# A hybrid decoder layer on one core: the up product by seven products in place of eight over half of its inner dimension

## What is computed

```python
def hybrid_layer(x, ...):
    ...                                        # projections, short convolution, attention, merge
    x = x + merged @ w_out
    f = rmsnorm(x, norm2_w) @ w_up             # the up product, 1024 -> 4096
    x = x + jnp.square(jax.nn.relu(f)) @ w_down   # the down product, 4096 -> 1024
    return x, new_conv, k, v
```

## Time and profile before

| | |
|---|---|
| median of 3 runs | 1617.1 us (1617.06 to 1617.59) |
| the profiled execution's own time | 1616.8 us |
| its span, first to last instruction | 1615.1 us |
| mean granted TensorE clock | 0.998 of 2.4 GHz |
| matmuls | 9776 |
| up product of a cycle | 23.72 us |
| down product of a cycle | 20.90 us |

### The profile page before, as it was taken

How to read it: one execution, slowest core, us unless ns; L and a number is a source line. 1 busy time by engine, 2 the same in 40 slices (tenths; PEclk the granted TensorE clock), 3 DMA queues, 4 the chain that set the end, 5 groups by cost and what they waited for, 6 DMA issues and landing times.

```text
span 1615.1 us, 25413 instructions
## 1 busy us (share of the span) xinstructions
PE 1600.1 (99%) x9776; PEld 1483.0 (92%) x9776; DVE 1059.5 (66%) x1411; ACT 530.9 (33%) x1044; POOL 720.7 (45%) x594
## 2 busy tenths in 40 slices
PE   9999999999999999999999999999999999999997
PEld 8999999999998888999988989999999999999996
DVE  7685977859612221356433587877777887787777
ACT  6655665555522221332134411111111111111123
POOL 5212121121222111223687486666666776666661
PEclk9999999999999999999999999999999999999999
DMA  4201112011184767363354111110011111111012
GB/s 165 68 27 55 54 40 68 27 41 54 41 283 149 233 221 238 118 232 104 122 189 144 53 53 52 53 53 26 27 53 53 52 53 53 53 53 53 27 40 111
DMA packets 133491, 144.99 MB, mean 90 GB/s; under 512 B 7839, under 2 KB 98619, under 8 KB 133372
## 3 DMA queue, kind: packets, MB, share of 16 engines
q1 hardware_dynamic: 133226, 143.34, 27.5%
q10 hardware_dynamic: 146, 0.04, 0.0%
HBM read 124.37 MB, written 18.98 MB: 89 GB/s over the span
## 4 chain that ended last, share of the span: by engine, by line
PE 85%; DVE 9%; ACT 3%; issue 1%; DMA 0%; DVEq 0%; ACTq 0%
PE ps L1289 51%; PE ps L1623 6%; PE ps L1625 6%; PE ps L1624 6%; DVE sp L2114 2%; PE ps L1580 2%; PE ps L1585 2%; PE ps L1583 2%; PE ps L1483 2%; DVE zc L2106 1%; PE ps L1439 1%; PE ps L1449 1%; PE ps L1527 1%; PE ps L1495 1%; ACT sp L1797 1%
## 5 line engine op out<-in xcount | busy, mean ns | idle before, releaser
L1289 PE MATMUL ps<-xh,wh 128*128 128x352 f32 (+1 forms) x956 | 322.6, 337 | 0.9 <-DVE xl L2087 0.7
L1289 PE MATMUL ps<-xh,wl 128*128 128x352 f32 (+1 forms) x956 | 312.7, 327 | 0.0
L1289 PE MATMUL ps<-xl,wh 128*128 128x352 f32 (+1 forms) x956 | 312.4, 327 | 0.0
L2243 DVE TENSOR_TENSOR x<-ps,x 128x1024 f32<-128x1024 f32 x210 | 257.1, 1224 | 42.8 <-PE ps L1625 23.9
L1140 POOL CAST wh<-raw 128x1024 fp32r<-128x1024 f32 x48 | 50.3, 1047 | 478.3 <-issue 205.4
L1289 PE MATMUL ps<-yh,wl 128*128 128x384 f32 (+1 forms) x768 | 250.6, 326 | 0.0
L1289 PE MATMUL ps<-yh,wh 128*128 128x384 f32 (+1 forms) x768 | 250.6, 326 | 0.0
L1289 PE MATMUL ps<-yl,wh 128*128 128x384 f32 (+1 forms) x768 | 250.3, 326 | 0.0
L1921 ACT ACTIVATE hf<-hf 128x384 f32<-128x384 f32 (+1 forms) x96 | 48.6, 508 | 554.7 <-DVE hf L2296 554.7
L1289 PEld LDWEIGHTS ps<-xh,wh 128*128 128x128 f32 x956 | 179.8, 188 | 17.2 <-issue 15.5
L1289 PEld LDWEIGHTS ps<-xl,wh 128*128 128x128 f32 x956 | 180.0, 188 | 0.7
(11 more groups left out here) (213 smaller groups left out, 3141.8 us busy)
## 6 DMA issues: line engine op xcount, KB each, us to landing
raw<-in_w_in SPq DMA_DIRECT2D x80, 256.0 KB, 3.3
...
```

The source lines that it names most:

```text
L1289: ins = mm(out, lhs[:, k * P:(k + 1) * P], rhs[:, x], start=(first and a == 0 and m == 0), stop=(last and a == n - 1 and m == 2))
L2243: V_.tensor_tensor(x, src, x, ALU.add).then_inc(step_free, 1)
```

## The change

Pairs 1 to 15 of the up product get a new form. Of the 8 K tiles, tiles 0 to 3 go by seven products in place of eight: the 2 x 2 of y is (K tiles 0-1, K tiles 2-3) x (first, second half of the prompt tokens), that of w_up is (tile of hidden channels) x (K tiles 0-1, 2-3). Tiles 4 to 7 stay plain, in chunks of 512 tokens, and the 64 sample tokens get matmuls of their own for all 8 tiles. Entries `("mix", n, m)`, m = 0 to 8, take the place of the six `("up", ...)`. A partial sum that several results need stays in its PSUM bank and goes on being added to (bank "x": mixes 0, 3, 5, 7; bank "z": mixes 2, 4); at four points ACT copies it to `hf` (`("keep", n, m)`), and `("join", n, m)` adds the bank of another mix to that copy on DVE; ACT then does relu and square, two instructions. Mix 8 and the end of mix 1 are the sample tokens, in bank 1.

The right operands (y and its four sums) are made once, behind the first pair: DVE writes y plain as well (`y_plain`), subtracts four times (`("twist",)`), ACT casts and DVE subtracts for the low parts (`("twist_low", k)`). The left operands are made by POOL for each pair: `up_op`, six slots of 512 columns, the four sums with twists of 256 elements each. The ring of five slots now holds the operands of both products, 6 of the pair ahead and 8 of the pair behind in turn. w_up comes in pairs of tiles, 512 KB a piece. Two buffers of sums take the place of four, so sums 2 and 3 wait for ACT's preps 3 and 2. Pair 0 stays plain, but its y now lies in pieces that end at token 512 and 1024, so matmuls that cross these are cut in two for K tiles 0 to 3.

The diff, cut to its core:

```diff
-                 ("up", 1, 2), ("relu", 1, 0), ("up", 0, 1), ("relu", 1, 2), ("up", 1, 1),
-                 ("relu", 0, 1), ("relu", 1, 1)]
+                 ("up", 1, 2), ("relu", 1, 0), ("twist",), ("up", 0, 1), ("relu", 1, 2), ("twist_low", 0), ("twist_low", 1),
+                 ("up", 1, 1), ("relu", 0, 1), ("twist_low", 2), ("relu", 1, 1), ("twist_low", 3)]
...
+        MIX_BANK = {"x": 4, "y": 5, "z": 6, "w": 0, "few": 1}
+        MIX = [("x", 0, None), ("y", 1, (0, 0)), ("z", 3, None), ("x", 2, None), ("z", 5, (0, 1)), ("x", 4, None), ("w", 6, (1, 0)),
+               ("x", None, (1, 1))]
+        KEEP = {0: (0, 0), 2: (1, 1), 3: (0, 1), 5: (1, 0)}
+        JOIN = {1: (0, 0), 4: (0, 1), 6: (1, 0), 7: (1, 1)}
+        W_PART = {0: (0, 0), 1: (0, 1), 3: (2, 0), 2: (2, 1), 5: (3, 0), 4: (3, 1), 6: (4, 1)}
+        W_PLAIN = (1, 5)
+        W_FEW = (0, 4)
+        U_LAST = (1, 4, 3, 5, 8, 8)
+        KEPT_FOR = {3: 1, 4: 2, 5: 3, 7: 4}
...
-            tail += [("sum", n - 1, k) for k in range(4)]
...
+            m = n - 1
+            tail += [("sum", m, 0), ("sum", m, 1), ("mix", n, 0), ("keep", n, 0), ("prep", m, 0), ("prep", m, "few0"), ("prep", m, "few1"),
+                     ("mix", n, 1), ("mix", n, 2), ("keep", n, 2), ("mix", n, 3), ("keep", n, 3), ("join", n, 1),
+                     ("prep", m, 1), ("prep", m, 6), ("mix", n, 4), ("mix", n, 5), ("keep", n, 5), ("prep", m, 3), ("prep", m, 4),
+                     ("join", n, 4), ("sum", m, 2), ("mix", n, 6), ("prep", m, 2), ("join", n, 6), ("sum", m, 3),
+                     ("mix", n, 7), ("prep", m, 5), ("join", n, 7), ("mix", n, 8), ("join", n, 8)]
...
+        def mix_bank_read(n, m):
+            if n == 1:
+                return read_no["up", 1, 1]
+            return read_no[(("prod", n - 2, 5, 0), ("prod", n - 2, 6, 0), ("prod", n - 2, 5, 1))[m] if m < 3 else ("prod", n - 2, 6, 0)]
...
             if p == 0 and q == 0:
-                return read_no["up", 2 * n + 3, 1]
+                return read_no["mix", n + 1, 8]
...
+        RING = []
+        for n in range(1, N_TWIN):
+            RING += [("u", n, x) for x in range(len(U_LAST))]
+            RING += [("d", n - 1, k) for k in range(N_OP)]
+        ring_no = {e: g for g, e in enumerate(RING)}
         def op_used(g):
-            n, k = divmod(g, N_OP)
-            return done_no[(OP_LAST[k][0], n, *OP_LAST[k][1:])]
+            kind, n, k = RING[g]
+            return done_no["mix", n, U_LAST[k]] if kind == "u" else done_no[(OP_LAST[k][0], n, *OP_LAST[k][1:])]
...
+            def load_pair(n):
+                if n == 1:
+                    sp_.wait_ge(w_split, 6 * NPAIR + 3 * KT + 2 + N_OUT + 2)
+                else:
+                    sp_.wait_ge(d_lo, ring_no["u", n - 1, len(U_LAST) - 1] + 1)
+                apart(sp_)
+                for s in range(2):
+                    sp_.dma_start(blocks(raw_u, 2 * P)[:, 4 * s:4 * s + 4, :], wup[:, 4 * s:4 * s + 4, ds(2 * n * P, 2 * P)]).then_inc(u_in, 16)
...
+            def slot_free(of):
+                if of < 2:
+                    pool.wait_ge(step_done, tile_end["up", 0])
+                elif of < N_RING:
+                    pool.wait_ge(step_done, tile_end["up", 1])
+                else:
                     pool.wait_ge(step_done, op_used(of - N_RING))
+                if of == N_RING - 1:
+                    pool.wait_ge(twist_lo, 4)
                 apart(pool)
...
+            def split_op(of, src, shape):
+                high, low = shape(w_hi_at[of % N_RING]), shape(w_lo_at[of % N_RING])
                 g.tensor_copy(high, src).then_inc(d_hi, 1)
                 pool.wait_ge(d_hi, of + 1)
                 g.tensor_tensor(low, src, f32(high), ALU.subtract).then_inc(d_lo, 1)
                 pool.wait_ge(d_lo, of + 1)
+            def up_op(n, x):
+                rows_ = blocks(raw_u, 2 * P)
+                a11, a12, a21, a22 = (rows_[:, KQ * j:KQ * j + KQ, i * P:i * P + P] for i in range(2) for j in range(2))
+                s1, s2, s4, s3 = (blocks(tw[t])[:, KQ * h:KQ * h + KQ, :] for t in range(2) for h in range(2))
+                of = ring_no["u", n, x]
+                if x == 0:
+                    pool.wait_ge(u_in, 32 * n)
+                slot_free(of)
+                if x == 2:
+                    twist(s1, a21, a22, ALU.add)
+                    twist(s2, s1, a11, ALU.subtract)
+                elif x == 3:
+                    twist(s3, a11, a21, ALU.subtract)
+                    twist(s4, a12, s2, ALU.subtract)
+                src = (rows_[:, 0:KT // 2, 0:P], rows_[:, KT // 2:KT, 0:P], blocks(tw[0]), blocks(tw[1]),
+                       rows_[:, 0:KT // 2, P:2 * P], rows_[:, KT // 2:KT, P:2 * P])[x]
+                split_op(of, src, blocks)
...
+            for n in range(N_OUT + 2):
                 tail_tile(n)
             for n in CYCLES:
+                for x in range(len(U_LAST)):
+                    up_op(n + 1, x)
+                for k in range(N_OP):
+                    if n == LAST_TWIN - 1 and k >= N_SOON:
...
+                    order_ = [*range(KT // 2, KT), *range(KT // 2)]
+                    for f in order_:
+                        pieces = y_pieces(f, a, z)
+                        for piece in pieces:
+                            out = bank(up_bank(j, c), piece[0] - a, piece[1] - a)
+                            for m, (w, part) in enumerate(((wh, 0), (wh, 1), (wl, 0))):
+                                ins = mm(out, w[n % 2][:, f * P:(f + 1) * P], y_at(f, part, *piece), start=(f == order_[0] and m == 0),
+                                         stop=(f == order_[-1] and m == 2), skip_group_check=True)
+                    ins.then_inc(step_done, 1)
+                elif e[0] == "mix":
+                    _, n, m = e
+                    def three(out, w, y, start, stop):
+                        for t, (high, part) in enumerate(((0, 0), (0, 1), (1, 0))):
+                            ins = mm(out, w[high], y[part], start=start and t == 0, stop=stop and t == 2, skip_group_check=True)
+                        return ins
+                    def weight(x, q):
+                        slot = ring("u", n, x)
+                        return [t[:, q * P:(q + 1) * P] for t in (w_hi_at[slot], w_lo_at[slot])]
+                    def samples(i):
+                        out = bank(MIX_BANK["few"], i * SMP, (i + 1) * SMP)
+                        for f in range(KT):
+                            x, q = (W_FEW[i], f) if f < KT // 2 else (W_PLAIN[i], f - KT // 2)
+                            ins = three(out, weight(x, q), [y_at(f, part, SEQ, NTOK) for part in range(2)], f == 0, f == KT - 1)
+                        return ins
+                    if m < len(MIX):
+                        where, p, over = MIX[m]
+                        out = bank(MIX_BANK[where])
+                        if m in (3, 4, 5, 7):
+                            pe.wait_ge(kept, 4 * (n - 1) + KEPT_FOR[m])
+                        else:
+                            pe.wait_ge(step_free, mix_bank_read(n, m))
+                        begun = where == "x" and m > 0 or (where == "z" and m > 2)
+                        if over:
+                            i, j = over
+                            pe.wait_ge(d_lo, ring_no["u", n, W_PLAIN[i]] + 1)
+                            for f in range(KT // 2, KT):
+                                ins = three(out, weight(W_PLAIN[i], f - KT // 2), [y_at(f, part, j * HS, (j + 1) * HS) for part in range(2)],
+                                            not begun and f == KT // 2, p is None and f == KT - 1)
+                            begun = True
+                        if p is not None:
+                            x, h = W_PART[p]
+                            pe.wait_ge(d_lo, ring_no["u", n, x] + 1)
+                            if n == 1 and p in TWIST_NO:
+                                pe.wait_ge(twist_lo, TWIST_NO[p] + 1)
+                            for q in range(KQ):
+                                ins = three(out, weight(x, KQ * h + q), [y_op[p][part][:, q * HS:(q + 1) * HS] for part in range(2)],
+                                            not begun and q == 0, q == KQ - 1)
+                        if m == 1:
+                            ins = samples(0)
+                    else:
+                        pe.wait_ge(d_lo, ring_no["u", n, W_FEW[1]] + 1)
+                        ins = samples(1)
...
+                elif e[0] == "twist":
+                    act.wait_ge(step_done, tile_end["up", 0])
+                    for k, p in enumerate(TWIST_OF):
+                        if k == 3:
+                            act.wait_ge(step_done, tile_end["up", 1])
+                        act.wait_ge(twisted, k + 1)
+                        A(y_op[p][0][:, :], y_plain[TWIST_IN[k]][:, :], ACT.Copy).then_inc(twist_hi, 1)
+                elif e[0] == "keep":
+                    _, n, m = e
+                    i, j = KEEP[m]
+                    if n >= 2 and m == 0:
```

(100 more changed lines are left out.)

162 lines of the change are left out of this document (84 added, 78 removed).

## The result

The changed kernel takes 1723.9 us (median of 4 runs) against 1617.1 for the kernel before: ratio 1.066, 95% interval 1.0647 to 1.0673. Forecast was 1697 with a range of 1648 to 1730. The direction, and 70 of the 80 us that the sum had, came as written; 36 us more came from a place that the sum had at nothing.

The account below looks back on a forecast made before the run. The prediction took TensorE (PE), busy 99%, to bound the kernel in 15 cycles of 44.62 us. Growth of 4.9 us a cycle (73.5 us) plus 6.5 us once made 80 us on 1616.8: 1697 us, range 1648 to 1730.

Parts of the forecast that it names:

- the sum: Whole kernel: 73.5 us over 15 cycles plus 6.5 us once, 80 us on 1616.8, giving 1697 us.
- Narrow matmuls by their load: PE's up product: 48 matmuls of 64 columns cost 112 ns each, their weight load; 25.83 us, 2.11 more than before.
- Rivals 3: Up product: narrow matmuls cost 40 ns by their columns, DVE's chain still makes PE wait; 1640 to 1670 us, chance 0.12.
- 4: Up product: narrow matmuls cost 40 ns by their columns and DVE's chain is hidden; faster, 1601 us, chance 0.06.
- The wait at product 0: Up product's end: PE, done at 25.83 us, waits 2.8 for DVE's list up to join 8; product 0 starts at 28.6.
- POOL fuller but not waited for: POOL's operand splits: about 38 us of work a cycle in place of 29.7, yet PE never waits for them.
- Once, 6.5 us: First pair of tiles: 3.5 us for cut matmuls and 3 us of mix 0 waiting for relu(1, 1).
- The cycle's 4.9 us: Each up/down cycle grows from product 0 starting at 28.6 in place of 23.7; x 15 is 73.5 us.
- PE's clock 1.00 in the cycles.: Expected sign in the profile: PE's granted clock stays full in the cycles.
- rival 5: Cycles: the clock falls to a mean of 0.95 with PE idle behind narrow matmuls; 36 us, 1733 us, chance 0.08.
- its upper end, 1730: Top of the forecast range; the case of DVE instructions stretched beside POOL, a 4.7 us wait a cycle, gave 1727.
- the line of the prediction: Price of one PE matmul: 13.6 ns + 0.4167 ns a column, so 40 ns for 64 columns, 1.93 us for 48.

Follow-up runs that it names:

- Experiments 4: The kernel before with only the tokens of up-product pairs 1 to 15 cut into 512, 512 and 64 instead of 384, 384 and 320: 1667.9 us, ratio 1.0313.
- 5: Kernel of 2 with the samples' high and low parts side by side, two narrow matmuls in place of three of 64 columns: 1636.4 us, ratio 1.0118.
- Experiment 1: The changed kernel with preps 3 and 4 moved ahead of mixes 4 and 5 and keep 5 in the list: 1676.2 us, ratio 1.036.
- 3: The changed kernel with nine more matmuls of 512 columns ahead of product 0, filling the pause: 1691.6 us, ratio 1.0459.
- 8: The kernel before with eight more DVE runs of the relu that product 0 waits for, a pause each cycle: 1667.7 us, ratio 1.0323.
- 9: The kernel of Experiments 4 with six more DVE runs of the relu that product 0 waits for: 1740.6 us, ratio 1.0765.
- kernels 7: The kernel before with seven more DVE runs of the relu that product 0 waits for, a pause each cycle: 1657.0 us, ratio 1.0242.
- 2: Kernel of Experiment 1 with the sample tokens' mix 8 and join 8 moved ahead of mix 7: 1661.6 us, ratio 1.0278.

## Why the prediction was right, and where it wasn't

- **Narrow matmuls by their load** (forecast 112 ns, up product 25.83 us). Right: 108 to 112 ns; the last narrow matmul starts 47.20 - 21.57 = 25.63 us after the first of the cycle. Experiments 4 and 5 show it apart from all else. Rivals 3 and 4, at 40 ns, are out. The Trainium skill (TensorE: Matmul & The Clock Gate, "LDWEIGHTS") has 107 ns for 128 columns; the traces agree for loads of 128 rows. The table under "Back-to-back issue gap" on that page, about 60 cycles up to 64 columns, is not what these matmuls take; the page gives it for a single matmul by itself and says that at few columns it counts too little for a stream of loads and matmuls.
- **The wait at product 0** (forecast start 28.6, wait 2.8). Right in place, order and size: 28.02, with 2.12 in the table of waits and 2.39 from last start to first. Experiment 1 removes it by a change of order alone. Inside the chain the terms differ and cancel: DVE's preps 3 and 4 took 2.74 us together (forecast 1.98), sums 2 and 3 took 1.18 and 0.67 (forecast 1.44 and 1.32):
```profile
1039.26 2.74 DVE L2521 TENSOR_TENSOR a_lo<-sum,a_hi 128x512 fp32r<-128x512 f32 x2 [2.96 <-ACT a_hi L2108]
...
1042.52 1.18 DVE L2513 TENSOR_TENSOR sum<-sum,hf 128x512 f32<-128x512 f32 x1
...
1045.94 0.67 DVE L2513 TENSOR_TENSOR sum<-hf,sum 128x512 f32<-128x512 f32 x1
```
  The cycle's 4.9 us came out as 4.3: 64.5 us for the 73.5 forecast.
- **POOL fuller but not waited for** (about 38 us). Right for the changed kernel: 38.01, and no row of PE waiting for it. In the faster versions it is late once, at the last pair, by 2.5 to 3.7 us.
- **Once, 6.5 us.** Right: 6.3, of it 2.7 for relu (1, 1) (forecast 3).
- **"PE's clock 1.00 in the cycles."** This step failed. The sum had the clock's cost at nothing; its fall stood as rival 5, with 0.08, as though it were another case than the forecast. It was a consequence of it: the pause that I forecast, behind the narrow matmuls that I forecast, is what brings the clock down (3, 8, 9). The price was right, 36 us forecast and measured, the mean clock 0.93 for 0.95. Added to the sum it would have given 80 + 36: 1733, nine over the result in place of 27 under. That 1723.9 lies in the range even so is in part luck: its upper end, 1730, stood for long instructions on DVE (a wait of 4.7 us), which didn't come, and without the slow clock the kernel would have taken some 1688. The Trainium skill (TensorE: Matmul & The Clock Gate, "HAM oscillation") warns of pauses in every turn of a loop; those it describes are waits for a transfer, longer than the 2.1 us here. The changed kernel loses the clock in every turn as the page has it, while kernels 7 and 8, with pauses in every turn as well, lose it in a few only.

What the change was to bring is real and small: six matmuls of 512 columns a cycle, 1.36 us. It needs quadrants of 512 tokens, and so leaves 64 sample tokens over, 48 matmuls that cost 5.2 us where the line of the prediction gives them 1.9. That exchange is why no version that does all the work has a shorter cycle than the kernel before, the best one included (44.97 for 44.62). Put right, the order gives back 62 of the 107 us (2), fewer loads 25 more (5), and 19 are left, 5 of them in the cycles and 14 once.

Left open: how much narrow work ahead of a pause, and how long a pause, the fall needs; experiments 1, 3, 7, 8 and 9 bound it only by these cases. What of the one-off 14 us of experiment 5 could be had back by another order at the last pair wasn't tried.
